# RWKV-7 recurrence on one core: one addition moved between VectorE's scans and differences, one scaling moved to ScalarE

## The chip, the cores and the metric

The kernel runs on one core of a Trainium2 chip. The metric is the device time of one execution in microseconds (us); the time of a kernel is the median of its runs.

## The reference

The program is a stack of six mixer blocks with mixture-of-experts or dense feed-forward parts behind them, all on 256 tokens of width 1024 in fp32. The part that matters here is the time mixing of the first block, a bidirectional RWKV-7 layer with 16 heads of width 64:

```python
w_log = -softplus(-(w0 + lora(xw, w1, w2, tanh))) - 0.5
decay = exp(-exp(w_log))
a     = sigmoid(a0 + lora(xa, a1, a2, identity))          # learning rates, per direction
k_dir = k[None] * (1.0 + (a - 1.0) * k_a)                 # keys scaled by them
b_dir = kk[None] * a
# per direction and head, over the tokens, forward and backward:
S_t = S_{t-1} (diag(w_t) + a_t^T b_t) + v_t^T k_t;   y_t = S_t r_t
```

The scan over tokens is computed in blocks of 64 tokens: decays become cumulative sums and exponentials of their differences, and the part inside a block needs the inverse of a unit triangular 64x64 matrix.

## The kernel before

A chunk is two heads (128 channels); there are eight of them. The loop `for s in range(-2, C + 2)` is written out once for each engine, and its pass is called a slot here. In slot s, five chunks are at five stages: e = s+2 (decays and learning rates out of the LoRA products), f = s+1 (features), c = s (the inverse), p = s-1 (the solve and the outputs), g = s-2 (normalisation). All engines run their instructions in the written order; they meet through semaphores. So the order within a slot is set by hand, on each engine for itself.

VectorE (`rwkv` under `block.vector`, L2263 to L2389). A slot with f in range begins with four cumulative sums (L2307, L2310: two forward, two backward, 128x128), waits for the last of them with `K(last)`, subtracts the block middle (L2313), forms 128x2 factors (L2314) and the third part `cx[:, 512:1024]` (L2315), which raises `rw_cc`. Then comes `level(c, 1)` (L2317), two 128x512 additions for z = 0 and 1, each of which waits for TensorE's `rw_XYt` and raises `rw_xy`. Then `solved_r(p, 0)` (L2319), two 64x128 additions that give tile R0 back to TensorE. After the mean's subtraction come `kkx`, `km = ea*ka + (1-ka)` (L2327, a `ts`), `km *= k` (L2328), `cum` (L2329), then `level(c, 2)`, and after the wait for `rw_E` the features, which raise `rw_feat`. At the end of the slot four masks are applied to the products of `ka0`, `ka1`, `kr0`, `kr1` (L2385, L2387).

TensorE (`rwkv`, L917). A slot runs `level_w(c,1)`, `solve_p(p,0)`, the mean, `level_xy(c,1)`, `solve_r(p,0)`, `level_w(c,2)` (waits for `rw_xy` of level 1, z by z), `solve_u(p,0)` (waits until VectorE has given R0 back), the product Zv (L1023), `level_xy(c,2)` (waits for ScalarE's copies Wb of level 2), and so on to level 5. `level_w` is L940, `level_xy` L953 and L958, `solve_r` L977, `solve_u` L987. At the slot's end stand y(p) (L1136 to L1141), bn(f) (L1146, reads `km`), `level_xy(c,5)`, and ka, kr (L1154). The `rw` products go through four PSUM tiles in turn: the sequence at the slot's end is g, y, bn, ka0, ka1, kr0, kr1, so kr0 takes the tile that y had and waits until ScalarE has copied y out.

ScalarE (`rwkv`, L1610). In a slot: copies Wb of level 1, the P0 copies, then `rw_cc` is waited for and three exponentials follow (L1645 to L1647), which raise `rw_E`; behind them the copies Wb of level 2, U0, Zv. At the end stand the decays and learning rates of chunk e (L1700 to L1702, which raise `rw_ea`), the logarithm and exponential of `ksq` (L1705, L1706) and the copy of y (L1709). L1510 and L1513 are the helpers through which all ScalarE operations go; L2082 (`tt`), L2085 (`ts`) and L2088 (`stt`) are those of VectorE.

Of the kernel before, what the change touches and what calls it, by code (L numbers as in the profile page):

```python
# [317 lines left out]
RWN = {}  # L318
# [132 lines left out]
def build(nc, d, out_d):  # L451
    ctx = ExitStack()
    with ctx:
# [30 lines left out]
        def col(name, j=0, n=1):  # L484
            return cols[:, COLS[name][0] + j:COLS[name][0] + j + n]
# [95 lines left out]
        def ev(name):  # L581
            if name not in named:
                named[name] = sem(name)
            return named[name]
# [7 lines left out]
        def ready(eng, g, m, plus=0):  # L592

            eng.wait_ge(tile_ready[g], m + 1 + plus)
# [905 lines left out]
        def _(act):  # L1500
# [8 lines left out]
            def fn(out, in_, f, scale=1.0, bias=0.0, **k):  # L1509
                return nc.scalar.activation(out, in_, f, scale=scale, bias=bias, **k)  # L1510
# [99 lines left out]
            def rwkv():  # L1610
# [22 lines left out]
                for s in range(-2, C + 2):  # L1633
                    e, f, c, p, g = s + 2, s + 1, s, s - 1, s - 2
                    on_e, on_f, on_c, on_p, on_g = e < C, 0 <= f < C, 0 <= c < C, 0 <= p < C, 0 <= g < C
                    if on_c:
                        level(c, 1)
                    if on_p:
                        solved("P", 0, p)
                    if on_f:  # L1640
                        if f:
                            act.wait_ge(ev("rw_pb"), f)
                        fn(rkr, rT[:, f, :], ACT.Copy, scale=col("rk", f))
                        act.wait_ge(ev("rw_cc"), f + 1)
                        K(fn(e3, cx[:, 0:512], ACT.Exp, scale=-1.0))  # L1645
                        fn(fac[f % 3], fac[f % 3], ACT.Exp)
                        fn(cx, cx, ACT.Exp).then_inc(ev("rw_E"), 1)  # L1647
                    if on_c:
                        level(c, 2)
                    if on_p:  # L1650
                        solved("U", 0, p)
                    if on_c:
                        let(copy(Zv[c % 2], got("Zv", c)), "Zv", c)
                    if on_p:
                        t = got("S", p)
                        for z in (0, 1):
                            for r in HALF:
                                last = fn(S0[r, z, r], t[r, 64 * z:64 * z + 64], ACT.Copy, scale=fac[p % 3][r, z:z + 1])
                        let(last, "S", p)
                    if on_g:  # L1660
                        act.wait_ge(ev("rw_d"), g + 1)
                        fn(sq, ys, ACT.Square).then_inc(ev("rw_sq"), 1)
                    if on_f:
                        let(copy(Vt[f % 3].rearrange("p j n -> p (j n)"), got("V", f)[:, 0:S]), "V", f)
                    if on_c:
                        level(c, 3)
                    if on_f:
                        for h in (0, 1):
                            copy(Ast[f % 2][:, h].rearrange("p z j t -> p (z j t)"), got(f"sm{h}", f)[:, 0:256]).then_inc(ev("rw_A"), 1)
                    if on_g:  # L1670
                        K(fn(sq, got("var", g), ACT.Ln, scale=1.0 / 64, bias=GN_EPS))
                        act.sem_inc(free("rw", RWN["var", g]), 1)
                        fn(sq, sq, ACT.Exp, scale=-0.5).then_inc(ev("rw_rs"), 1)
                    if on_e:
                        act.wait_ge(ev("rw_feat"), e)
                        fn(ksq, kT[:, e, :], ACT.Square, scale=col("kk", e)).then_inc(ev("rw_ksq"), 1)
                    if on_f:
                        let(copy(BK[f % 2].rearrange("p z i n -> p (z i n)"), got("BK", f)), "BK", f)
                    if on_p:
                        solved("P", 1, p)  # L1680
                    if on_c:
                        level(c, 4)
                    if on_p:
                        solved("U", 1, p)
                    if on_e:
                        for z in (0, 1):
                            t = got(f"wa{z}", e)
                            for i in (0, 1):
                                b = 16 * i + 8 * z + e
                                last = fn(ea[:, (2 * i + z) * S:(2 * i + z + 1) * S], t[:, i * S:(i + 1) * S], ACT.Exp, scale=-1.0,  # L1690
                                          bias=neg0[:, b:b + 1])
                            let(last, f"wa{z}", e)
                    if on_f:
                        for h in (0, 1):
                            let(copy(N6[f % 2][:, h].rearrange("p j t -> p (j t)"), got(f"n6{h}", f)[:, 0:P]), f"n6{h}", f)
                    if on_c:
                        level(c, 5)
                    if on_e:
                        act.wait_ge(free("rw", RWN["wa1", e]), RWN["wa1", e] // 4 + 1)
                        K(fn(ea, ea, ACT.Ln, bias=1.0))  # L1700
                        fn(ea[:, 0:512], ea[:, 0:512], ACT.Exp, scale=-1.0, bias=-0.5)
                        fn(ea[:, 512:1024], ea[:, 512:1024], ACT.Exp, scale=-1.0).then_inc(ev("rw_ea"), 1)  # L1702
                    if on_e:
                        act.wait_ge(ev("rw_kkm"), e + 1)
                        K(fn(ksq, ksq, ACT.Ln))  # L1705
                        fn(ksq, ksq, ACT.Exp, scale=-0.5).then_inc(ev("rw_kkn"), 1)  # L1706
                    if on_p:
                        act.wait_ge(ev("rw_n2"), p)
                        let(copy(ys, got("y", p)), "y", p)  # L1709
# [360 lines left out]
        def _(dve):  # L2070
# [4 lines left out]
            def K(ins, it=None, per=0):  # L2075

                own[0] += 1
                ins.then_inc(chain, 1)
                dve.wait_ge(chain, own[0] if it is None else it * per + own[0])

            def tt(out, a, b, op):
                return v.tensor_tensor(out, a, b, op)  # L2082

            def ts(out, a, s1, s2, o1, o2=ALU.bypass):
                return v.tensor_scalar(out, a, s1, s2, o1, o2)  # L2085
# [177 lines left out]
            def rwkv():  # L2263
# [10 lines left out]
                def both(a):  # L2274
                    return a[:, None, :].to_broadcast([P, 2, S])

                def two(a):
                    return a.rearrange("p (z s) -> p z s", z=2)

                def level(c, lev):  # L2280
                    for z in (0, 1):
                        dve.wait_ge(ev("rw_XYt"), rw_at(c, lev, z))
                        a = XY[c % 3][:, z].rearrange("p x n -> p (x n)")[:, 0:512 if lev < RW_LEVELS else 256]
                        tt(a, ps[:, 2 + z, 0:512 if lev < RW_LEVELS else 256], a, ADD).then_inc(ev("rw_xy"), 1)
# [13 lines left out]
                for s in range(-2, C + 2):  # L2298
# [4 lines left out]
                    if on_f:  # L2303
                        dve.wait_ge(ev("rw_ea"), f + 1)
                        for j in range(2):
                            o, i_ = (a[:, 0:S][:, j * P:(j + 1) * P] for a in (cum, ea))
                            v.tensor_tensor_scan(o, ones, i_, 0.0, MUL, SUB)  # L2307
                        for j in range(2):
                            o, i_ = (a[:, S:2 * S][:, j * P:(j + 1) * P] for a in (cum, ea))
                            last = v.tensor_tensor_scan(o[:, ::-1], ones, i_[:, ::-1], 0.0, MUL, SUB)  # L2310
                        K(last)
                        c4, cc4 = (a[:, 0:512].rearrange("p (q t) -> p q t", q=4) for a in (cum, cx))
                        K(tt(cc4, c4, c4[:, :, 63:64].to_broadcast([P, 4, P]), SUB))  # L2313
                        tt(fac[f % 3], cx[:, 127:385:257], cum[:, 191:320:128], ADD)  # L2314
                        tt(cx[:, 512:1024], cx[:, 0:512], ea[:, 0:512], ADD).then_inc(ev("rw_cc"), 1)  # L2315
                    if on_c:
                        level(c, 1)  # L2317
                    if on_p:
                        solved_r(p, 0)  # L2319
# [4 lines left out]
                    if on_f:  # L2324
                        dve.wait_ge(ev("rw_kkn"), f + 1)
                        stt(kkx, kT[:, f, :], col("kk", f), ksq, MUL, MUL)
                        K(ts(km, ea[:, 512:1024], col("ka", f), omka[:, f:f + 1], MUL, ADD))  # L2327
                        tt(two(km), two(km), both(kT[:, f, :]), MUL)  # L2328
                        K(stt(two(cum), both(kkx), float(2 ** 20), two(ea[:, 512:1024]), MUL, MUL))  # L2329
                    if on_c:  # L2330
                        level(c, 2)
# [649 lines left out]
```

## Time and profile before

| | value |
|---|---|
| median of 3 runs | 3011.99 us (3011.68 to 3012.53) |
| profiled execution | 3007.85 us, span 3006.0 us |
| TensorE busy | 2821.6 us, 94% of the span |
| VectorE busy | 2053.1 us, 68% |
| ScalarE busy | 1626.8 us, 54% |
| GpSimd busy | 159.5 us, 5% |
| mean granted TensorE clock | 0.969 of full speed |

The busy shares are over the whole program; the recurrence is only the stretch from about 155 to 466 us of it. What the changed instructions are worth has to be read inside a slot. The chain of waits is the one view that goes back from the last instruction and names at each step what released it; the timelines list an engine's instructions in order, merged where neighbours are alike, with the idle time before a row and its releaser in brackets.

### The profile page before, as it was taken

How to read it: one execution, taken by the hardware profiler on the slowest of the kernel's cores; microseconds unless marked ns; L12 is line 12 of the kernel's file. 1: busy time of each engine (PE TensorE's matmuls, PEld its weight loads, DVE VectorE, ACT ScalarE, POOL GpSimd, SP SyncE). 2: the span in 40 equal slices, each digit the busy share in tenths (PEclk: the TensorE clock that was granted, in tenths of full speed). 3: DMA queues.
4: the chain of work that ended last, by engine and by line, in shares of the span. 5: the costliest groups of instructions: out<-in, count | busy, mean ns of one | idle time of the engine just before them, and what ended most of it. 6: DMA issues, size and time to landing. Idle time of an engine off the chain costs nothing.

```text
span 3006.0 us, 54400 instructions
## 1 busy us (share of the span) xinstructions
PE 2821.6 (94%) x22799; PEld 2552.2 (85%) x22799; DVE 2053.1 (68%) x2555; ACT 1626.8 (54%) x2318; POOL 159.5 (5%) x164
## 2 busy tenths in 40 slices
PE   6879998999998999899998989998999989999999
PEld 5867777778778999877886889998899879997999
DVE  7768875899985656599997655555555775556554
ACT  2445543788883444388886544445444734445443
POOL 0034420000000112000000000000000000000000
PEclk8989998999998999899999999999999999999999
DMA  8501123699984644199997404444354304443353
GB/s 325 217 2 59 59 73 137 248 357 352 358 337 181 224 183 182 57 352 356 355 352 264 183 18 173 184 158 154 113 182 182 141 29 170 183 157 135 127 181 126
DMA packets 78263, 572.85 MB, mean 191 GB/s; under 512 B 8802, under 2 KB 8802, under 8 KB 9186
## 3 DMA queue, kind: packets, MB, share of 16 engines
q1 hardware_dynamic: 76752, 558.93, 50.1%
q10 hardware_dynamic: 1298, 10.90, 0.9%
q8 instruction: 157, 2.57, 0.3%
q14 instruction: 56, 0.46, 0.0%
HBM read 568.74 MB, written 1.05 MB: 190 GB/s over the span
## 4 chain that ended last, share of the span: by engine, by line
PE 84%; DVE 11%; ACT 3%; issue 1%; DMA 1%; POOL 0%; DVEq 0%; SPq 0%; ACTq 0%; PEldq 0%
PE ps L1298 14%; PE ps L1222 12%; PE ps L835 9%; PE ps L836 9%; PE ps L837 9%; PE ps L1319 7%; DVE arena L2088 4%; DVE hl L2082 1%; DVE wl L2082 1%; DVE arena L2082 1%; PE ps L858 1%; PE ps L857 1%; PE ps L856 1%; PE ps L1392 1%; PE ps L953 1%; PE ps L879 1%
## 5 line engine op out<-in xcount | busy, mean ns | idle before, releaser
L2082 DVE TENSOR_TENSOR wl<-ring,wh 128x1024 fp32r<-128x1024 f32 (+1 forms) x560 | 937.7, 1696 | 487.8 <-ACT wh L1513 481.5
L1513 ACT ACTIVATE wh<-ring 128x1024 fp32r<-128x1024 f32 (+1 forms) x560 | 788.7, 1431 | 512.7 <-PE ps L837 308.5
L835 PE MATMUL ps<-hh,wh 128*128 128x256 f32 x2464 | 714.6, 290 | 51.3 <-DVE hl L2082 41.8
L836 PE MATMUL ps<-hh,wl 128*128 128x256 f32 x2464 | 704.0, 286 | 0.0
L837 PE MATMUL ps<-hl,wh 128*128 128x256 f32 x2464 | 703.7, 286 | 0.0
L835 PEld LDWEIGHTS ps<-hh,wh 128*128 128x128 f32 x2464 | 479.9, 195 | 62.4 <-issue 42.7
L836 PEld LDWEIGHTS ps<-hh,wl 128*128 128x128 f32 x2464 | 480.0, 195 | 3.1 <-issue 2.9
L837 PEld LDWEIGHTS ps<-hl,wh 128*128 128x128 f32 x2464 | 479.8, 195 | 0.0
L1222 PE MATMUL ps<-hidh,wh 128*128 128x256 f32 x1024 | 290.2, 283 | 0.0
L1222 PE MATMUL ps<-hidh,wl 128*128 128x256 f32 x1024 | 289.8, 283 | 0.0
L1222 PE MATMUL ps<-hidl,wh 128*128 128x256 f32 x1024 | 289.8, 283 | 0.0
L1513 ACT ACTIVATE arena<-ps 128x512 f32<-128x512 f32 (+3 forms) x158 | 86.9, 550 | 306.7 <-PE ps L837 192.6
L1510 ACT ACTIVATE arena<-arena 128x256 f32<-128x256 f32 (+7 forms) x420 | 206.0, 495 | 57.3 <-DVE arena L2632 15.2
L1298 PE MATMUL ps<-wh,parts 128*128 128x512 f32 x656 | 225.5, 405 | 1.2 <-DVE parts L2082 1.2
L1298 PE MATMUL ps<-hh,parts 128*128 128x512 f32 x624 | 210.9, 399 | 0.0
L1222 PEld LDWEIGHTS ps<-hidh,wh 128*128 128x128 f32 x1024 | 196.6, 192 | 0.8 <-DVE hidl L2082 0.8
L1222 PEld LDWEIGHTS ps<-hidh,wl 128*128 128x128 f32 x1024 | 196.6, 192 | 0.0
L1222 PEld LDWEIGHTS ps<-hidl,wh 128*128 128x128 f32 x1024 | 196.6, 192 | 0.0
L2082 DVE TENSOR_TENSOR hl<-ring,hh 128x1024 fp32r<-128x1024 f32 x160 | 189.8, 1220 | 4.4 <-ACT hh L1513 3.9
L1513 ACT ACTIVATE hh<-ring 128x1024 fp32r<-128x1024 f32 x160 | 168.2, 1061 | 35.1 <-PE ps L1298 30.2
L2088 DVE SCALAR_TENSOR_TENSOR arena<-ps,arena 128x512 f32<-128x512 f32 (+4 forms) x134 | 81.1, 619 | 117.8 <-PE ps L837 81.4
L1298 PEld LDWEIGHTS ps<-wh,parts 128*128 128x128 f32 x656 | 123.4, 188 | 28.3 <-issue 2.0
(259 smaller groups left out, 4603.4 us busy)
## 6 DMA issues: line engine op xcount, KB each, us to landing
ring<-in_stream SPq DMA_DIRECT2D x532, 1024.0 KB, 4.9
arena<-in_wcmp ACTq DMA_DIRECT2D x2, 2048.0 KB, 10.2
arena<-in_lora ACTq DMA_DIRECT2D x1, 2048.0 KB, 9.8
arena<-in_atm ACTq DMA_DIRECT2D x1, 1762.0 KB, 7.4
x<-in_xT ACTq DMA_DIRECT2D x1, 1024.0 KB
out<-x SPq DMA_DIRECT2D x1, 1024.0 KB, 3.9
arena<-in_rwm ACTq DMA_DIRECT2D x1, 736.0 KB, 12.8
cols<-in_cols ACTq DMA_DIRECT2D x1, 715.0 KB
```

The source lines that it names most:

```text
L835: mm(out, w[0], h[0], start=first, stop=False)
L836: mm(out, w[1], h[0], start=False, stop=False)
L837: return mm(out, w[0], h[1], start=False, stop=last)
L856: mm(o, a[0], W[0][:, k, :], start=k == 0, stop=False)
L857: mm(o, a[1], W[0][:, k, :], start=False, stop=False)
L1222: last = mm(o, W[a][:, f, c * P:(c + 1) * P], H[b][:, f, :], start=False, stop=False, skip_group_check=True)
L1298: last = mm(t, h[a][:, k, :], w[c][:, k, :], start=part == 0 and k == 0 and n == 0, stop=part == 1 and k == 3 and n == 2)
L1319: last = mm(t[n], h[a][:, f, :], w[c][:, f, 512 * n:512 * n + 512], start=e % INNER == 0 and f == 0 and j == 0, stop=e % INNER == INNER - ...
L1510: return nc.scalar.activation(out, in_, f, scale=scale, bias=bias, **k)
L1513: return nc.scalar.activation(out, in_, ACT.Copy)
L2082: return v.tensor_tensor(out, a, b, op)
L2088: return v.scalar_tensor_tensor(out, a, s, b, o1, o2)
```

## The change

On VectorE, in slots with both a chunk f and a chunk c, the two additions of `level(c, 1)` stand between the four cumulative sums and the subtraction L2313; the completion of the last sum is waited for behind them instead of ahead of them. The `ts` of L2327 leaves VectorE. ScalarE computes `ea*ka + (1-ka)` for chunk e instead, directly behind the exponentials that give `ea`, a slot earlier: it waits for its own exponentials, and, where there is a chunk f, until TensorE has finished bn(f), which is the last reader of the old `km`. The multiplication by k stays on VectorE.

```diff
@@ ScalarE, rwkv
                         fn(ea[:, 512:1024], ea[:, 512:1024], ACT.Exp, scale=-1.0).then_inc(ev("rw_ea"), 1)
+                        act.wait_ge(ev("rw_ea"), e + 1)
+                        if on_f:
+                            ready(act, "rw", RWN["bn", f])
+                        K(fn(km, ea[:, 512:1024], ACT.Identity, scale=col("ka", e), bias=omka[:, e:e + 1]))
                     if on_e:
                         act.wait_ge(ev("rw_kkm"), e + 1)
@@ VectorE, rwkv
                             last = v.tensor_tensor_scan(o[:, ::-1], ones, i_[:, ::-1], 0.0, MUL, SUB)
-                        K(last)
+                        own[0] += 1
+                        last.then_inc(chain, 1)
+                        if on_c:
+                            level(c, 1)
+                        dve.wait_ge(chain, own[0])
                         c4, cc4 = (a[:, 0:512].rearrange("p (q t) -> p q t", q=4) for a in (cum, cx))
                         K(tt(cc4, c4, c4[:, :, 63:64].to_broadcast([P, 4, P]), SUB))
                         tt(fac[f % 3], cx[:, 127:385:257], cum[:, 191:320:128], ADD)
                         tt(cx[:, 512:1024], cx[:, 0:512], ea[:, 0:512], ADD).then_inc(ev("rw_cc"), 1)
-                    if on_c:
+                    if on_c and not on_f:
                         level(c, 1)
@@
                         stt(kkx, kT[:, f, :], col("kk", f), ksq, MUL, MUL)
-                        K(ts(km, ea[:, 512:1024], col("ka", f), omka[:, f:f + 1], MUL, ADD))
-                        tt(two(km), two(km), both(kT[:, f, :]), MUL)
+                        K(tt(two(km), two(km), both(kT[:, f, :]), MUL))
```

## Rows read from the trace of the kernel before

**Rows 1.** The page: the chain that ended last, by engine.
```profile
PE 84%; DVE 11%; ACT 3%; issue 1%; DMA 1%; POOL 0%; DVEq 0%; SPq 0%; ACTq 0%; PEldq 0%
```
**Rows 2.** Windows view, one slot (s = 4): busy per engine, clock, DMA.
```profile
309.76:345.86 36.10, 33.77 (x726) 27.64 (x726) 30.65 (x49) 18.66 (x47) 16.05 (x14) 1.00 0.19 61
```
**Rows 3.** Chain of waits through the turn to slot 4: start us, us, what.
```profile
306.48 1.06 PE ps L1146 x2
...
309.76 1.27 DVE under L2082 x2
...
312.28 1.22 DVE under L2307 x2
...
314.17 0.70 DVE under L2082
...
315.66 0.61 DVE arena L2082
...
317.98 1.93 PE ps L1023 x16
319.91 0.61 PE ps L953 x16
```
**Rows 4.** Timeline of VectorE in slot 4: solved_r, the ts, level 2.
```profile
316.89 0.59 DVE L2082 TENSOR_TENSOR arena<-ps,spare 64x128 f32<-64x128 f32 x2
...
318.73 0.54 DVE L2085 TENSOR_SCALAR under<-under,cols,small 128x512 f32<-128x512 f32 x1
...
321.11 0.69 DVE L2082 TENSOR_TENSOR arena<-ps,arena 128x512 f32<-128x512 f32 x1 [0.52 <-PE ps L958]
```
**Rows 5.** Timeline of TensorE in slot 4: end of level_xy(1), then level_w(2).
```profile
313.81 0.63 PE L958 MATMUL ps<-arena,under 64*64 64x64 f32 x16
...
315.15 0.22 PE L958 MATMUL ps<-arena,under 64*64 64x64 f32 x1
...
316.41 1.28 PE L940 MATMUL ps<-arena 64*64 64x64 f32 x32 [0.97 <-DVE arena L2082]
```
**Rows 6.** Timeline of ScalarE, end of slot 3 and start of slot 4.
```profile
303.46 3.05 ACT L1510 ACTIVATE under<-under 128x1024 f32<-128x1024 f32 x5
306.73 0.60 ACT L1513 ACTIVATE spare<-ps 128x512 f32<-128x512 f32 x1 [0.22 <-DVEq L2379]
...
312.97 0.51 ACT L1510 ACTIVATE under<-arena,cols 128x256 f32<-128x256 f32 x1
315.69 0.63 ACT L1510 ACTIVATE under<-under 128x512 f32<-128x512 f32 x1 [2.22 <-DVE under L2082]
...
317.53 0.66 ACT L1513 ACTIVATE under<-ps 128x256 f32<-128x256 f32 x2
```
**Rows 7.** Timeline of ScalarE, short window: the last exponential of `ksq`.
```profile
306.09 0.42 ACT L1510 ACTIVATE under<-under 128x256 f32<-128x256 f32 x1
```
**Rows 8.** Timeline of TensorE in slot 1: level_w(2).
```profile
209.67 1.97 PE L940 MATMUL ps<-arena 64*64 64x64 f32 x32 [2.18 <-DVE arena L2082]
```
**Rows 9.** Timeline of VectorE in slot 1: solved_r.
```profile
210.16 0.59 DVE L2082 TENSOR_TENSOR arena<-ps,spare 64x128 f32<-64x128 f32 x2
```
**Rows 10.** Windows view in slot 1: the columns as in rows 2.
```profile
210.00:212.00 2.00, 2.00 (x40) 1.88 (x36) 1.92 (x6) 1.47 (x3) 0.00 (x0) 0.50 0.00 0
```
**Rows 11.** Chain of waits, slots 0 and 1.
```profile
183.37 0.61 PE ps L953 x16
...
212.07 2.43 PE ps L1023 x16
```
**Rows 12.** Timeline of TensorE in slot 0: level_w(2).
```profile
180.16 1.28 PE L940 MATMUL ps<-arena 64*64 64x64 f32 x32 [2.44 <-DVE arena L2082]
```
**Rows 13.** Timeline of ScalarE in slot 0: copies Wb of level 2.
```profile
181.16 0.70 ACT L1513 ACTIVATE under<-ps 128x256 f32<-128x256 f32 x2
```
**Rows 14.** Timeline of ScalarE in slot -1: the exponential that raises rw_E.
```profile
159.47 1.04 ACT L1510 ACTIVATE under<-under 128x1024 f32<-128x1024 f32 x1
```
**Rows 15.** Timeline of VectorE in slot -1: first feature, which waits for rw_E.
```profile
160.88 0.69 DVE L2082 TENSOR_TENSOR arena<-arena,under 128x512 f32<-128x512 f32 x1
```

## The prediction

> **What bounds the kernel now.** I read the page first, for the chain that ended last: TensorE holds 84% of it and VectorE 11% [rows 1]. So most of VectorE's work is beside the path, and only the places where the chain is on VectorE can pay. The windows view then gives one slot of the recurrence: 36.10 us, of which TensorE is busy 33.77 us and VectorE 30.65, at a granted clock of 1.00 and a DMA share of 0.19 [rows 2]. Nothing is short but the order: TensorE idles 2.3 us in a slot, and the question is where. The chain of waits answers it. It is on TensorE up to 309.76, then on VectorE without a gap through masks, sums, subtraction, the third part and the first addition of level 1, until TensorE takes level_w(2) at 316.41; from there it is TensorE's product Zv (317.98) and level_xy(2) (319.91) [rows 3, 5]. TensorE had stood idle 0.97 us before 316.41 [rows 5]. That is the stall which the reordering addresses: level 1 stands behind 1.5 us of subtraction and additions (314.17 to 315.66) [rows 3] that TensorE does not wait for.
>
> **The ends of the stall.** In slot 4 the four sums end at about 314.15, 0.02 before the subtraction starts [rows 3]. TensorE's level_xy(1) has finished z = 0 at 313.81 + 0.63 = 314.44 and z = 1 at 315.15 + 0.22 = 315.37 [rows 5]. So in the new place level 1 does not run freely: its z = 0 can start at 314.5 and its z = 1 at 315.45. VectorE, which has no idle time here now, gets two gaps, 0.35 and about 0.3 us (315.45 against 314.5 + 0.61 = 315.11, an addition being 0.61 in the chain [rows 3]).
>
> **Part 1, slots 2 to 6 (five of them).** level_w(2) can start its z = 0 at about 315.4 and its z = 1 at 316.3 and end at 316.9, where it now ends at 316.41 + 1.28 = 317.69 [rows 5]: 0.8 us gained. But behind it on TensorE stands solve_u, which needs R0, and R0 is given back by solved_r on VectorE, which ends at 316.89 + 0.59 = 317.48 now [rows 4]. That is already only 0.2 us ahead of the end of level_w(2). solved_r is queued behind subtraction, factors, third part and both additions of level 1 in either order, so it gains nothing by the change and loses the two new gaps. I work it through: z = 1 from 315.45; the subtraction 0.61 later, 316.06; from the subtraction to the end of the third part it is 315.66 - 314.17 = 1.49 [rows 3], so 317.55; solved_r 0.59 (to 318.1). solve_u therefore starts at about 318.15 and Zv 0.3 later (317.98 - 317.69 now) at 318.45, against 317.98. The slot gets 0.5 us longer by this, where the stall seemed to promise 0.8 to 1.0 shorter. The bounds: if the gaps on VectorE were absorbed (its ends are modelled to 0.1 us), 0; if level_w(2) alone set Zv, -0.8.
>
> What stays covered: the third part ends at 317.55 instead of 315.66, so ScalarE's exponentials start 1.9 us later and the copies Wb of level 2, queued behind them, start at 317.53 + 1.9 = 319.4 [rows 6] and have the first half by 319.8. level_xy(2) wants it at 319.91 + 0.5 = 320.4. 0.6 us to spare; if this cover went, each 0.1 us beyond would cost the slot 0.1. rw_E comes at about 319.4, and its reader stands behind level 2, after 321.97.
>
> **Part 2, the ts off VectorE.** It is 0.54 us in every slot [rows 4]. It stands ahead of level 2, and level 2 already waits 0.52 us there for TensorE [rows 4]. Removing it only makes that wait 1.1 us: worth 0 in slots 0 to 6 (a gain of its own would need VectorE to be late at level 2, and it is early). In slot -1 there is no level 2 between, so the feature starts earlier, up to the point where rw_E holds it: 159.47 + 1.04 = 160.51 against 160.88 [rows 14, 15], so 0.3 us once.
>
> **Part 3, the scaling on ScalarE.** A 128x512 exponential takes 0.63 without pointer operands, and a 128x256 operation takes 0.51 with one pointer operand against 0.42 without [rows 6, 7]; so 0.63 + 2 x 0.09 = 0.81 us with scale and bias from memory. ScalarE's three exponentials of `ea` end about 0.75 us ahead of 306.51 (303.46 + 3.05), at 305.8 [rows 6]. Then it must wait for bn, which ends at 306.48 + 1.06 = 307.54 [rows 3]. Queued behind the wait are the two operations on `ksq` and the copy of y. The scaling ends at 308.4, the two take 0.78 (to 309.2), the copy of y 0.60 [rows 6], to 309.8, where it ended at 307.33. Its reader is kr0, which takes y's tile: TensorE begins it right when ka ends, 309.76 [rows 3]. So the cover of 2.4 us is used up exactly. I take 0.2 us a slot: 0.1 late and 0.1 for a weight load that can no longer run ahead. Bounds 0 and 0.5 (if the scaling takes 1.1 us). The new path from kr over level_w(1) and level_xy(1) to level 1 has no slack any more, so these 0.2 us are paid in full, on top of 0.5. The slots whose kr they touch are 2 to 6 again.
>
> The Trainium skill, "ScalarE: Activation LUTs", section "What ACT_TABLE_LOAD costs", gives a 128-row operation with immediate operands 186 ns + 0.833 ns per column and 93 ns for each pointer operand, which would be 0.80 us here; by it the sum stays the same. No row of before has both operands as pointers at this width.
>
> **Slots 0 and 1.** Slot 1 has no mean product, so level_xy(1) is ready before the sums end and level 1 runs at once. R0 comes at 210.16 + 0.59 = 210.75 in either order [rows 9], but level_w(2), which started at 209.67 and took 1.97 us at half clock [rows 8, 10], is done before it. Zv can start at 210.75 + 0.3 = 211.1 instead of 212.07 and takes between 1.93 and 2.43 us, by clock [rows 3, 11]: a gain of 0.9 to 1.5, I take 1.2. In slot 0 there is no R0; what holds level_xy(2) is ScalarE: Wb is copied from 181.16 [rows 13], and 1.3 us later (two additions stand ahead of the third part now) that gives 182.45, its first half 182.85, so 182.95 instead of 183.37 [rows 11]: 0.4 gained.
>
> **The sum.** -0.3 (slot -1) - 0.4 (slot 0) - 1.2 (slot 1) + 5 x (0.5 + 0.2) = +1.6 us. All other slots are as before, and the work behind the recurrence is TensorE's and starts by that much later. Against the profiled 3007.85 us this is 3009.4; the median of the runs is 4.1 us above the profiled execution, and I keep that distance: 3011.99 + 1.6 = 3013.6.
>
> **Rivals.** (A) R0 is not what holds Zv, as the chain view would have it, which names only level_w(2) ahead of Zv. Then slots 2 to 6 gain 0.8 each less 0.2 for kr: -1.9 - 3.0 = -4.9, or -5.9 with kr hidden: 3006.1 to 3007.1. For it speaks that the chain does not pass through R0; against it that R0 has only 0.2 us of lead and is moved later. 0.13, and 0.05 of that at beyond -6 us.
>
> (B) The granted clock falls. In slot 1 TensorE idled 2.18 us and then ran at a granted clock of 0.50, that is 1.2 GHz instead of 2.4: level_w(2) 1.97 against 1.28 us, Zv 2.43 against 1.93 [rows 3, 5, 8, 10, 11], about 1.3 us with solve_u. In slot 0 it idled 2.44 us and kept its clock [rows 12]. By my working, slots 2 to 6 go from 0.97 us of idle time to about 0.3 + 1.2 = 1.5 in two pieces. If that brings the clock down in each, 5 x 1.3 = 6.7 more: 3020.3, slower. It decides from four slots on (3018.8). 0.12. The Trainium skill, "TensorE: Matmul & The Clock Gate", section "Part 1: The HAM clock gate", says the clock depends on how busy TensorE has been of late; rows 8 and 10 agree with it, rows 12 show that an idle stretch of this size does not always do it.
>
> (C) The reordering does nothing measurable: gaps and gains inside the modelled ends, -1.9 + 1 to + 2, 3011 to 3012. 0.2. My forecast, with its own range 3012.3 to 3015.5, has 0.55.
>
> **Range and chances.** A measurement of this kernel can tell 0.2%, 6.0 us, from no change. Leaving out the far ends of A and B, 3007.0 to 3018.5. Faster by over 0.2% (below 3006.0): 0.06. Slower (above 3018.0): 0.11. Within: 0.83.
>
> **What would show it.** Right: in slots 2 to 6 VectorE waits for TensorE's L958 before each of the two additions of level 1, solved_r ends some 0.6 us later after the sums than before, solve_u (L987) is released by VectorE with 1 us of idle time ahead, level 2 on VectorE waits about 1.1 us, the copy of y ends just about when ka does, and a slot takes 36.7 to 36.8 us. Wrong: a slot shorter than 36.1, Zv directly behind level_w(2), a clock below 1.00 in slots 2 to 6, or copies Wb of level 2 that hold level_xy(2).

## The result, and the profile after

The changed kernel takes 3021.67 us (median of 7 runs, 3018.14 to 3025.32), the kernel before 3011.99 (7 runs, 3007.74 to 3013.97). The ratio is 1.0034, with a 95% interval of 1.0025 to 1.0043: slower by 0.34%, about 10 us. The profiled execution took 3019.32 us (span 3017.5) and its mean granted clock is 0.964, against 0.969.

The windows view of the changed kernel, one row for each slot from 2 to 6, cut where TensorE starts kr. Columns as in rows 2: stretch, its length, busy time (and count) of TensorE, its weight loads, VectorE, ScalarE, GpSimd, then clock, DMA share, GB/s.

```profile
235.40:272.21 36.81, 33.90 (x727) 27.63 (x727) 30.30 (x48) 19.47 (x48) 16.04 (x14) 1.00 0.18 60
272.21:312.14 39.93, 37.01 (x726) 30.68 (x727) 30.29 (x48) 19.48 (x48) 16.04 (x14) 0.91 0.16 55
312.14:351.35 39.21, 36.85 (x727) 30.39 (x727) 29.94 (x48) 19.48 (x48) 16.06 (x14) 0.91 0.16 56
351.35:388.16 36.81, 33.90 (x727) 27.63 (x727) 30.29 (x48) 19.46 (x48) 16.05 (x14) 1.00 0.17 60
388.16:426.34 38.18, 35.32 (x716) 29.79 (x717) 30.07 (x47) 13.98 (x37) 14.15 (x14) 0.91 0.15 53
```

Two things are in it. A slot at clock 1.00 takes 36.81 us against 36.10 [rows 2], together the 0.5 + 0.2 of the sum. And in three of the five slots the clock is 0.91 in the mean, and these are 2.4 to 3.1 us longer. In what follows, a fall is a stretch in which the granted clock goes from 1.00 to 0.50. (Slot 6 has less in it than the others: 34.40 us before, from 382.04 to 416.44, and 35.05 with the change in the experiment e3 below, where it has no fall.)

Where the 0.71 us are, on VectorE in slot 2:

```profile
240.05 0.69 DVE L2086 TENSOR_TENSOR arena<-ps,arena 128x512 f32<-128x512 f32 x1 [0.35 <-PE ps L958]
240.98 0.69 DVE L2086 TENSOR_TENSOR arena<-ps,arena 128x512 f32<-128x512 f32 x1 [0.24 <-PE ps L958]
...
243.10 0.59 DVE L2086 TENSOR_TENSOR arena<-ps,spare 64x128 f32<-64x128 f32 x2
...
247.33 0.69 DVE L2086 TENSOR_TENSOR arena<-ps,arena 128x512 f32<-128x512 f32 x1 [0.95 <-PE ps L958]
```

The first two rows are level 1 in its new place. Each waits for TensorE's L958, 0.35 and 0.24 us; before, it did not wait at all. The third row is solved_r, which answers to rows 4, and the last is level 2, whose wait has grown from 0.52 to 0.95 us: this is where the removed `ts` went. TensorE in the same slot:

```profile
235.40 1.16 PE L1154 MATMUL ps<-arena,under 64*128 64x128 f32 x16 [0.18 <-ACT spare L1513]
...
241.82 0.68 PE L940 MATMUL ps<-arena 64*64 64x64 f32 x16 [0.25 <-DVE arena L2086]
243.75 0.45 PE L987 MATMUL ps<-arena 64*64 64x64 f32 x8 [1.24 <-DVE arena L2086]
```

kr starts 0.18 us behind the end of ka (234.83 + 0.39 = 235.22), held by ScalarE's copy of y. That is less of a delay than it looks, since before, with nothing to wait for, kr started 0.12 us behind ka (309.32 + 0.39 = 309.71, then 309.83; the kernel before at the turn to slot 4, from two short windows of the timeline):

```profile
309.32 0.39 PE L1154 MATMUL ps<-arena,under 64*128 64x128 f32 x4
309.83 1.16 PE L1154 MATMUL ps<-arena,under 64*128 64x128 f32 x16
```

level_w(2) is done at 241.82 + 0.68 = 242.5, 7.3 us behind the end of ka, where it was 7.9 before [rows 3, 5], and then solve_u (L987) waits 1.24 us for VectorE, for R0. Where before there was one idle stretch of 0.97 us there are now two, 0.25 and 1.24. In slot 3 this is followed by (windows view with columns as above in stretches of 2 us, then the chain of waits):

```profile
280.00:282.00 2.00, 1.44 (x13) 1.37 (x14) 1.74 (x5) 1.94 (x4) 0.00 (x0) 0.73 0.03 8
282.00:284.00 2.00, 2.00 (x12) 2.00 (x11) 1.13 (x2) 0.95 (x4) 0.00 (x0) 0.50 0.00 0
284.00:286.00 2.00, 2.00 (x31) 1.88 (x32) 0.00 (x0) 0.60 (x1) 0.00 (x0) 0.50 0.00 0
286.00:288.00 2.00, 2.00 (x44) 1.93 (x42) 0.69 (x1) 0.00 (x0) 0.00 (x0) 0.56 0.04 8
```

```profile
281.01 3.61 PE ps L1023 x16
284.62 1.05 PE ps L953 x16
...
287.37 0.72 PE ps L958 x16
```

The granted clock stands at 0.50, which is 1.2 GHz, through Zv and level_xy(2). Zv takes 3.61 us instead of 1.93, the first part of level_xy(2) 1.05 instead of 0.61 [rows 3].

The account of the profiled executions: kr of slot 2 starts at 235.40, where it started at 237.62 before (2.2 gained in slots -1 to 1); slots 2 to 5 cost 0.71 each and slot 6 0.65 (35.05 against 34.40) without the clock, 3.5 in all; the three falls cost 3.1 + 2.4 + 3.1 = 8.6. That is +9.9, and the work behind the recurrence starts at 476.33 instead of 466.43. The remaining 1.6 us between the two profiled executions lie behind the recurrence, in code that is the same.

### The profile page after: what moved, and what is told of

The parts are those of the page before. It is cut to its first block, busy times and chain, and to the rows that moved or that the text cites. A ratio compares the mean times of both kernels' runs of the same rounds, so it can differ in the third digit from the quotient of the medians.

```text
span 3017.5 us, 54415 instructions
## 1 busy us (share of the span) xinstructions
PE 2834.6 (94%) x22799; PEld 2566.7 (85%) x22799; DVE 2051.4 (68%) x2547; ACT 1633.0 (54%) x2326; POOL 159.5 (5%) x164
## 3 DMA queue, kind: packets, MB, share of 16 engines
HBM read 568.74 MB, written 1.05 MB: 189 GB/s over the span
## 4 chain that ended last, share of the span: by engine, by line
PE 84%; DVE 10%; ACT 3%; issue 1%; DMA 1%; DVEq 0%; SPq 0%; ACTq 0%; PEldq 0%
PE ps L1298 14%; PE ps L1222 12%; PE ps L835 9%; PE ps L836 9%; PE ps L837 9%; PE ps L1319 7%; DVE arena L2092 4%; DVE wl L2086 2%; PE ps L858 1%; PE ps L857 1%; PE ps L856 1%; PE ps L1392 1%; DVE hl L2086 1%; DVE arena L2086 1%; PE ps L953 1%; ACT arena L1510 1%
## 5 line engine op out<-in xcount | busy, mean ns | idle before, releaser
L2086 DVE TENSOR_TENSOR arena<-ps,arena 128x512 f32<-128x512 f32 (+2 forms) x145 | 88.1, 622 | 93.3 <-PE ps L958 35.1
```

## The experiments

Each was run beside the kernel before on the same chip. Ratios are to that kernel, with 95% intervals; its median was 3013.14 us beside the first four and 3014.14 beside the other four. Each trace is of one execution.

**e1_scaling_only**: the scaling goes to ScalarE, level 1 keeps its old place.

```diff
+                        act.wait_ge(ev("rw_ea"), e + 1)
+                        if on_f:
+                            ready(act, "rw", RWN["bn", f])
+                        K(fn(km, ea[:, 512:1024], ACT.Identity, scale=col("ka", e), bias=omka[:, e:e + 1]))
...
-                        K(ts(km, ea[:, 512:1024], col("ka", f), omka[:, f:f + 1], MUL, ADD))
-                        tt(two(km), two(km), both(kT[:, f, :]), MUL)
+                        K(tt(two(km), two(km), both(kT[:, f, :]), MUL))
```

> Only the scaling of the learning rates goes to ScalarE; level 1 keeps its place behind the third part. Theory (the 9.7 us that the whole change costs are made of 0.5 to 0.7 us a slot for R0 and kr, and mostly of a fall of TensorE's granted clock in some of slots 2 to 6 behind the longer idle stretch ahead of solve_u): here R0 is not delayed by gaps on VectorE, so no fall in slots 2 to 6; kr starts 0.2 to 0.3 us behind the end of ka instead of at once, VectorE's kr masks 0.1 later, a slot of 36.2 us against 36.1, slot 1 falls to 0.50 as before: about 0.5 us above before, 3012 to 3013. Rival (the wait of kr for the copy of y is what lets the clock fall, or a part of the excess is the new operation on ScalarE): falls in slots 2 to 6, 3017 or more.

Measured: 3011.49 us, ratio 1.0002 (0.9993 to 1.0011). Slot 1 has its fall, slots 2 to 6 have none, and a slot is 36.16 us (275.59 to 311.75, start of kr to start of kr). The chain of waits goes through ScalarE:

```profile
308.34 1.07 PE ps L1146 x2
309.50 0.82 ACT under L1510
310.34 0.43 ACT under L1510
...
311.12 0.59 ACT spare L1513
311.75 1.21 PE ps L1154 x16
```

bn, the scaling (0.82 us), the two operations on `ksq`, the copy of y, kr. The queue behind the wait for bn is just what part 3 of the prediction lists. It costs 0.06 us a slot: kr starts 0.18 us behind ka here too, where it started 0.12 behind it without the wait. So the rival, that the scaling carries the excess, is out.

**e2_level_only**: only level 1 moves; the scaling stays on VectorE.

```diff
-                        K(last)
+                        own[0] += 1
+                        last.then_inc(chain, 1)
+                        if on_c:
+                            level(c, 1)
+                        dve.wait_ge(chain, own[0])
...
-                    if on_c:
+                    if on_c and not on_f:
                         level(c, 1)
```

> Only level 1 moves between the sums and the subtraction; the scaling stays on VectorE. Theory: in slots 2 to 6 VectorE waits 0.35 and 0.25 us for level_xy(1), solve_u comes 0.5 us later behind an idle stretch of some 1.2 us, a slot without a fall of the clock takes 36.6 us, and the clock falls to 0.50 in some of slots 2 to 6, at 2.4 to 3.1 us each: 3016 to 3021, most of what the whole change costs. Rival (the scaling carries the cost): 3013 without a fall in slots 2 to 6.

Measured: 3023.15 us, ratio 1.0033 (1.0021 to 1.0044), as much as the whole change. Slot 3, with the clock at 1.00, takes 36.76 us (281.00 to 317.76); slots 2, 4 and 5 take 39.2 to 39.9, with Zv at 2.7 to 3.6 us, and here slots 0 and 1 have a fall too. So the moved level 1 alone does it. The slot's size was expected at 36.6 and is 36.76: the R0 term is 0.66 us and not 0.5. The chain shows from what:

```profile
323.35 0.69 DVE arena L2082
324.04 0.61 DVE under L2082
...
325.78 0.29 DVE arena L2082
326.11 0.45 PE ps L987 x8
326.56 3.60 PE ps L1023 x16
```

solve_u takes 0.45 us on the path when it starts from idle, where I had 0.3 for it.

**e3_busy**: the whole change, and in the idle stretch before solve_u two products that nothing reads.

```diff
                     if on_c:
                         level_w(c, 2)
+                    if on_c and on_p:
+                        for i in range(2):
+                            mm(ps[:, 2 + i % 2, 0:S], ones, mats[:, 0:S], start=True, stop=True, skip_group_check=True)
```

> The whole change, and two products of 128x128 by 128x256 that nothing reads between level_w(2) and solve_u on TensorE in slots 1 to 7 (1.06 us, into banks that are free then). It computes the same. Theory (the clock falls because TensorE idles there): the clock is 1.00 in slots 2 to 6, each takes 36.8 to 36.9 us, and the time is that of my sum without rival B, 3013 to 3014.5. Rival (the clock falls for another reason, or each matmul added just makes the slot longer): falls remain and the time is 3021 or above.

Measured: 3013.22 us, ratio 0.9999 (0.9990 to 1.0008). Two slots of it in the windows view, and TensorE's timeline:

```profile
272.32:309.13 36.81, 34.95 (x730) 28.31 (x730) 30.30 (x48) 19.45 (x48) 16.05 (x14) 1.00 0.17 60
309.13:345.94 36.81, 34.96 (x730) 28.31 (x730) 29.94 (x48) 19.45 (x48) 16.04 (x14) 1.00 0.17 60
```

```profile
316.17 1.13 PE L1014 MATMUL ps<-mats 128*128 128x256 f32 x4
317.49 0.45 PE L987 MATMUL ps<-arena 64*64 64x64 f32 x8 [0.18 <-DVE arena L2089]
```

TensorE does more work, solve_u waits for the same R0, the slot has the same 36.81 us, and the clock stays at 1.00 in all slots from 0 to 6. All that is gone in these slots are the falls, and with them the whole slowdown. This settles the cause of the miss: the idle stretch of 1.24 us was what let the clock fall. (kr of slot 7 starts at 417.81 instead of 426.34. Behind it this trace has a long fall of its own, from 453.6 to 463.8 us, so the work behind the recurrence starts at 470.76 instead of 476.33; the medians of the change and of e3 are 8.5 us apart.)

**e4_r0_first**: the whole change and three orders more (shown cut; for the end of the slot on ScalarE, the lines as they stand afterwards).

```diff
@@ VectorE
                         if on_c:
                             level(c, 1)
+                            if on_p:
+                                solved_r(p, 0)
                         dve.wait_ge(chain, own[0])
...
-                    if on_p:
+                    if on_p and not (on_c and on_f):
                         solved_r(p, 0)
@@ ScalarE
+                        if on_c:
+                            level(c, 2)
                         act.wait_ge(ev("rw_cc"), f + 1)
...
-                    if on_c:
+                    if on_c and not on_f:
                         level(c, 2)
@@ ScalarE, end of the slot: copy of y ahead of the scaling
                         K(fn(ksq, ksq, ACT.Ln))
+                    if on_p:
+                        act.wait_ge(ev("rw_n2"), p)
+                        let(copy(ys, got("y", p)), "y", p)
+                    if on_e:
+                        act.wait_ge(ev("rw_ea"), e + 1)
+                        if on_f:
+                            ready(act, "rw", RWN["bn", f])
+                        K(fn(km, ea[:, 512:1024], ACT.Identity, scale=col("ka", e), bias=omka[:, e:e + 1]))
+                        fn(ksq, ksq, ACT.Exp, scale=-0.5).then_inc(ev("rw_kkn"), 1)
```

> The whole change, with three orders more: VectorE's solved_r directly behind level 1, ahead of the subtraction; ScalarE's copies Wb of level 2 ahead of the three exponentials; the copy of y ahead of the scaling. Theory (R0 behind the subtraction is what turned the gain into a loss): solve_u follows level_w(2) at once, Zv starts 0.8 us earlier than before, level 2 on VectorE is then held by VectorE itself (0.1 to 0.4 late), a slot of 35.3 to 35.5 us at clock 1.00 in slots 2 to 6: 3006 to 3008. Rival (what holds the slot is elsewhere, level 2 or the exponentials): a slot of 36.1 or more and 3010 to 3013.

Measured: 3002.61 us, ratio 0.9965 (0.9951 to 0.9979), faster than both kernels. A slot takes 35.56 us and the clock is 1.00 in slots 0 to 6. TensorE and VectorE in slot 4:

```profile
310.71 0.68 PE L940 MATMUL ps<-arena 64*64 64x64 f32 x16 [0.25 <-DVE arena L2089]
311.24 0.45 PE L987 MATMUL ps<-arena 64*64 64x64 f32 x8
```

```profile
310.60 0.59 DVE L2089 TENSOR_TENSOR arena<-ps,spare 64x128 f32<-64x128 f32 x2
...
315.28 1.29 DVE L2089 TENSOR_TENSOR arena<-ps,arena 128x512 f32<-128x512 f32 x2
```

solved_r follows level 1, solve_u follows level_w(2) without a wait, and the gain that the reordering promised is there. Level 2 (the last row) has no wait before it any more: TensorE had its first half at 314.07 + 0.63 = 314.70, VectorE comes at 315.28. The bound has gone over to VectorE. The time is 3 us lower than I expected, and 10.5 us lower than the kernel before beside it (3013.14). Of these the traces show 5.4 in the recurrence: kr of slot 2 starts 4.5 us earlier (233.14 against 237.62), slots 2 to 6 give 2.7 more, and 1.8 are lost again behind them, where the clock is at 0.50 from 444 to 454 us. Where the other 5 us come from is not shown.

**e5_r0_only**: the whole change with solved_r behind level 1 alone (the VectorE hunk of e4).

> The whole change with one order more: VectorE's solved_r directly behind level 1. ScalarE's copies Wb of level 2 stay behind the exponentials. Theory (two queues hold the gain, VectorE's with R0 and ScalarE's with Wb): Zv starts 0.8 us earlier than before, but Wb comes 0.6 us later than in the whole change, since the third part does, so level_xy(2) waits about 1.1 us for ScalarE behind Zv and a slot is 36.7 to 36.8 us again, with or without falls of the clock, 3013 to 3022. Rival (R0 alone was the cause): a slot of 36.0 or less, 3008 or less.

Measured: 3016.26 us, ratio 1.0005 (0.9995 to 1.0015). Slots of 36.75 us with the clock at 1.00 (311.79 to 348.54), 38.2 and 38.1 in slots 3 and 5, which have a fall; slots 1 and 6 have one too. Each of the four falls lasts 3.4 us. TensorE and ScalarE in slot 4:

```profile
318.74 0.45 PE L987 MATMUL ps<-arena 64*64 64x64 f32 x8
319.12 2.00 PE L1023 MATMUL ps<-spare,under 128*128 128x64 f32 x16
322.39 0.68 PE L953 MATMUL ps<-under,arena 64*64 64x64 f32 x16 [1.27 <-ACT under L1513]
```

```profile
320.12 0.63 ACT L1510 ACTIVATE under<-under 128x512 f32<-128x512 f32 x1 [4.69 <-DVE under L2086]
...
321.95 0.66 ACT L1513 ACTIVATE under<-ps 128x256 f32<-128x256 f32 x2
```

solve_u no longer waits, Zv starts earlier, and then level_xy(2) waits 1.27 us for the copies Wb, which stand on ScalarE behind exponentials that wait 4.69 us for the third part. The gain was held by two queues in a row, and freeing one hands the stall to the other, with the clock's falls behind it as before.

**e6_r0_first_ts**: e4 with the scaling back on VectorE (and its four lines on ScalarE taken out).

```diff
-                        K(tt(two(km), two(km), both(kT[:, f, :]), MUL))
+                        K(ts(km, ea[:, 512:1024], col("ka", f), omka[:, f:f + 1], MUL, ADD))
+                        tt(two(km), two(km), both(kT[:, f, :]), MUL)
```

> All orders of e4_r0_first, but the scaling km = ea*ka + (1-ka) stays on VectorE as one 0.54 us operation ahead of level 2. Theory: once level 1 and R0 come first, VectorE reaches level 2 later than TensorE (0.6 us late in e4_r0_first), so these 0.54 us are on the path: a slot of 36.1 us instead of 35.56, 5 to 6 slots, 3005 to 3006. Rival (the operation is covered here too, as it was in the kernel before): 35.56 and 3002 to 3003.

Measured: 3005.07 us, ratio 0.9963 (0.9949 to 0.9977). A slot takes 36.02 us (269.19 to 305.21) against 35.56: 0.46 us for an operation that was worth nothing in the kernel before. The times of e4 and e6 don't tell the two apart; the slots do.

**e7_y_last**: e4 with the scaling ahead of the `ksq` operations and the copy of y, as in the whole change.

> All orders of e4_r0_first but one: the scaling stands ahead of the operations on ksq and the copy of y, as in the whole change. Theory: kr waits for the copy of y again, a slot of 35.75 us instead of 35.56, 1 us in all, 3003 to 3004.5. Rival (the wait is hidden): 35.56.

Measured: 3002.46 us, ratio 0.9955 (0.9938 to 0.9972). A slot takes 35.61 us (268.95 to 304.56), so the wait of kr costs 0.05, less than the 0.2 I expected. The gap between ka and kr is 0.18 us in the trace again, and in e4 it is 0.12 without a wait. Neither guess is right, and in time it is nothing.

**e8_before_busy**: the kernel before, with three products that nothing reads in slot 1's idle stretch.

```diff
+                    if c == 1:
+                        for i in range(3):
+                            mm(ps[:, i % 2, 0:S], ones, mats[:, 0:S], start=True, stop=True, skip_group_check=True)
                     if on_c:
                         level_w(c, 2)
```

> The kernel before with three products of 128x128 by 128x256 that nothing reads ahead of level_w(2) in slot 1 alone, inside its 2.18 us of idle time. It computes the same. Theory (an idle stretch is what lets the clock fall): the clock stays at 1.00 from 205 to 216 us, level_w(2) there takes 1.28 us instead of 1.97 and Zv 1.93 instead of 2.43, and what follows comes about 1.3 us earlier. Rival: the fall stays.

One run, 3007.20 us. In slot 1 the clock stays up and both products have their full speed, but slot 0, which comes earlier and is untouched, has a fall in this execution:

```profile
182.00:184.00 2.00, 2.00 (x11) 1.95 (x10) 0.50 (x1) 0.00 (x0) 0.00 (x0) 0.50 0.00 0
...
212.00:214.00 2.00, 1.95 (x44) 1.89 (x45) 1.93 (x5) 1.95 (x5) 0.00 (x0) 1.00 0.00 0
```

```profile
212.05 1.28 PE L940 MATMUL ps<-arena 64*64 64x64 f32 x32 [0.69 <-DVE arena L2085]
213.18 0.45 PE L987 MATMUL ps<-arena 64*64 64x64 f32 x8
213.56 2.00 PE L1026 MATMUL ps<-spare,under 128*128 128x64 f32 x16
```

level_w(2) takes 1.28 us instead of 1.97 [rows 8]. Slot 1, from ka to ka, is 33.20 us (204.25 to 237.45) against 34.52 before (201.88 to 236.40): the 1.3 us expected. Slot 0 shows that the same idle stretch (2.43 us here, 2.44 in rows 12) has a fall in one execution and none in another.

## Why the prediction was right or wrong

The sum without the clock was right in its parts. The gaps of level 1 were forecast at 0.35 and 0.3 us and are 0.35 and 0.24; the wait of solve_u for R0 was forecast and is 1.24 us; the copy of y ends 0.12 us behind ka and kr waits for it; the `ts` turned into waiting at level 2; slots -1 to 1 gained 2.2 us, 1.9 forecast (slots -1 and 0 together 0.8 for 0.7, slot 1 1.4 for 1.2, since its Zv ran at the full clock). Two terms were off and cancelled: R0 costs 0.66 us a slot and not 0.5 (e2), since solve_u starting from idle takes 0.45 us on the path and not 0.3, and the late kr costs 0.05 and not 0.2 (e1, e7, and 36.81 against 36.76), since 0.12 of its 0.18 us behind ka were there before. That the two errors cancel is luck. e3, in which slots 0 to 6 of the change run without falls, measures 0.9999 (0.9990 to 1.0008), where the sum said 1.0005; the interval holds both.

What failed is the step from idle time to clock, rival B. It was named with its mechanism and its place and given 0.12, and it is what happened. Its own figure, 3020.3 us, is near the measured time only because it had five falls at 1.3 us where there were three at 2.9. Three steps of it were wrong.

Its chance. I held 1.5 us of idle time in two pieces against 2.18 us with a fall and 2.44 us without, and read the second as a sign that 1.5 would rarely do. The traces show that the clock falls behind the same stretch in some slots and executions and not in others (of slots 2 to 6, in 3, 4 and 6 with the change and in 2, 4 and 5 in e2; slot 0 in e8 but not before, where it is the same code). One stretch without a fall was no evidence of safety; what did count was that before, with 0.97 us, none of slots 2 to 6 had one, and none has one in the traces of e1 and e8, which have the same stall there.

Its price. 1.3 us came from slot 1 [rows 8 to 11], and I took it for the price of any fall. What differs is how long the clock stays low. In slot 1 it was at 0.50 for 3.4 us, from 209.7 to 213.1: 0.92 in the mean of 208 to 210, 0.50 from 210 to 212 [rows 10], 0.73 from 212 to 214:

```profile
208.00:210.00 2.00, 0.33 (x6) 0.36 (x8) 1.97 (x5) 1.01 (x3) 0.00 (x0) 0.92 0.00 0
...
212.00:214.00 2.00, 2.00 (x15) 2.00 (x14) 0.93 (x2) 0.61 (x3) 0.00 (x0) 0.73 0.00 0
```

The three falls of the changed kernel last 6.8 us each (in slot 3 from 281.0 to 287.8). Two cost 3.1 us; the one in slot 4 costs 2.4, probably because its last 1.4 us lie behind level_xy(2), which ends at 327.26, where a slot at full clock waits for VectorE. The falls of e5 last 3.4 us again and cost 1.4 to 1.5 (38.1 and 38.2 against 36.75). Nothing here shows why one fall lasts 3.4 us and another 6.8; the trace of e2 has both.

Its point. With 1.3 us a fall I needed four falls for a slowdown beyond 0.2%; at 2.9 us, two are enough. The high end of the range, 3018.5, followed from the small price, and the measured 3021.67 lies above it. The point estimate was 8 us too low for this one cause.

Rival A, that R0 does not hold Zv, is out by the 1.24 us row. Rival C, nothing measurable, has the time that e3 shows for the change without its falls, but not the reason: a slot is 0.71 us longer, and the gaps on VectorE are there. The cover of the copies Wb, given as 0.6 us, held in the whole change (0.7: the first half is copied at 244.94 + 0.38, level_xy(2) starts at 246.05) and was gone as soon as R0 was early (e5), as the price stated for it said.

## What to carry to other kernels

An operation moved ahead in an in-order queue helps little if the engine that waits for it waits next for something that still stands behind it. Here that was R0, which had come only 0.2 us ahead of its use before, and after R0 the copies Wb on the other engine; follow the waiting engine's next two instructions before moving anything, and move those too (e4: 0.9965).

When a reordering trades one idle stretch of TensorE for a longer one, price a fall of its clock by the work behind the new stretch, run at half speed, and by more than the shortest fall in the trace: 3.4 us at the low clock cost 1.3 to 1.5 us here, 6.8 cost 2.4 to 3.1. Give the fall a large chance when any slot of the trace shows one. Work that nothing reads, put into the stretch, tells in one run whether the clock is the cause (e3).

## What the runs showed of the hardware that I had not expected

Behind an idle stretch of 1.24 us, with 0.25 us of idle time shortly before it, the granted clock went from 1.00 to 0.50 in slots 3, 4 and 6 of one execution, and not in slots 2 and 5, which have the same two stretches, nor in slot 1, which has 0.63 and 1.24 us. With products in the stretch it went down in none of them (e3). In slot 3 it was at or near 0.50 from 281 to 288 us although TensorE was busy all the time from 280.6 on.

The falls seem to differ between executions of one kernel; no kernel was traced twice, but slot 0 has a fall in e8 and none in the kernel before, with the same code up to there. The changed kernel's seven runs spread over 7.2 us at mean granted clocks of 0.962 to 0.966.

The scaling with two operands from memory took 0.82 us, against 0.63 for an exponential of that size with none; the estimate was 0.81. The Trainium skill, "ScalarE: Activation LUTs", section "What ACT_TABLE_LOAD costs", would give 0.80, and the trace agrees.
